# Reciprocal root of q, k and the convolution's norm as an exponential of a logarithm, in a hybrid conv / attention / expert block

## The chip, the core and the metric

The kernel runs on one core of one Trainium2 chip. The metric is the device time of one execution in microseconds, the median of several runs. One core has five engines that run their own instruction queues and meet at semaphores: PE (matrix products; PEld is its loading of weights), DVE (vectors), ACT (activations), POOL, and SP, which here only issues DMAs. Reads and writes of the on-chip tiles are fast; `bank` tiles are the eight accumulation banks that PE writes.

## What is computed

One layer of a streaming encoder over 512 tokens of width 2048, all in f32. Cut to what matters here:

```python
h   = rmsnorm(x, norm1_g) * (1 + scale1) + shift1
a   = h @ w_in
# group A: GLU -> causal depthwise conv(31) -> layernorm -> silu, 1024 channels
h   = conv(val * sigmoid(gate)) + dw_b
y   = (h - mean(h)) * rsqrt(var(h) + EPS);  conv_out = silu(y * g + b)
# group B: 8 heads; q and k are 128 plain columns and 64 rotary columns per head
q = rmsnorm(q, q_norm_g);  k = rmsnorm(k, k_norm_g)     # x * rsqrt(mean(x*x) + EPS) * g
q, k = rope(q), rope(k)
p = softmax(mask(q @ k.T * 192**-0.5));  attn_out = p @ v
x = x + gate1 * (concat[conv_out, attn_out] @ w_out)
# then: norm, product-key search for 16 of 16384 experts in each of 8 heads,
# gelu(x . u) of the experts chosen, and the weighted sum of their v rows
```

## The kernel before

Features lie on partitions and tokens along a row, so most tiles are 128x512. Each f32 product is made of three passes on PE: a weight tile `w_raw` comes by DMA, ACT copies it to `w_hi` (L430), DVE subtracts to get `w_lo` (L761), and PE multiplies `w_hi` by the high and low part of the activations and `w_lo` by the high part (L1294, L1295, L1296). The order of the work is written out by hand for each engine; nothing reorders it, and every wait is a semaphore in the code.

The stages follow each other: modulation vectors and the first norm, the input projection, the convolution's taps on DVE, the values and rotary parts, then the **attention stage** (from 545 to 790 us of the span), the output projection, the expert keys, and from there to the end the stream of all expert weights. The change touches the attention stage alone.

Its start (call it the prelude): PE sums the convolution's channels into `bank3`, projects q and k of head 0 (`project`), sums the squares of q and k across partitions with a product with ones (`sum_squares`, L1394, L1396, L1398), projects head 1, sums the squares of the centred convolution (L1460), and then the squares of q and k of head 1. After each sum ACT takes a square root (`root_of`, L544, for q as r = 0 and k as r = 1; L595 for the convolution) and DVE the reciprocal (`norm_of`, L922; L1000 for the convolution, late), and multiplies `q_n`, `q_r`, `k_n` and `k_r` by it (L924, L927, L930). PE may overwrite the bank of q only after `q_used`, which `q_n` sets.

Then one **head** after another, eight of them. In each, PE writes the scores of four query blocks (L1411, L1412), DVE takes the row maximum (L936 to L938), ACT the exponential (L554), DVE the division by the sum (L944), PE transposes the result (L1418), DVE copies the transposed block out of `bank7` (L951), but the fourth block is copied by ACT (L572), and PE multiplies the values by the whole (`weigh_values`, L1426), which ACT copies to `att_o` (L576). Between the blocks of heads 1 to 6 (in order of time) PE projects q and k of the head two further on. At the end of each of these six heads ACT does `root_of(0)`, then the copy L572 for which `weigh_values` waits, then `root_of(1)`, then L576:

```python
root_of(0, v, j)
act.wait_ge(tr_ready, ...)
act.activation(prob_t[:, :, 3 * P:4 * P], bank[7]..., ACT.Copy)   # L572
root_of(1, v, j)
act.wait_ge(pv_ready, ...)
act.activation(att_o[:, u + i * 2, :], bank[4][:], ACT.Copy)      # L576
```

DVE does the norm of q at the very end of a head and the norm of k after the first block of the next. The last two heads have no projection; the seventh still has a norm of k.

ACT holds the tables of one set of functions at a time. Where the next function is in another set, an ACT_TABLE_LOAD stands ahead of it, put there when the program is built.

Of the kernel before, what the change touches and what calls it, by code (L numbers as in the profile page):

```python
# [9 lines left out]
ALU = mybir.AluOpType  # L10
ACT = mybir.ActivationFunctionType
# [11 lines left out]
CONV_CH, CONV_W = 1024, 31  # L23
# [4 lines left out]
NLAT = KQ + KKV  # L28
# [57 lines left out]
def build(nc, x_d, c_d, pos_d, prm_d, wada_d, win_d, wqr_d, wval_d, whd_d, wout_d, wwq_d, keys_d, u_d, v_d, urow_d, out_d):  # L86
# [4 lines left out]
    with ExitStack() as ctx:  # L91
# [10 lines left out]
        bank = [ctx.enter_context(nc.psum_tensor(f"bank{i}", [P, T], F32)) for i in range(8)]  # L102
# [22 lines left out]
        qr_rot = at("qr_rot", 194, [P, 4, T])  # L125
        cos_t = at("cos_t", 204, [P, T])
        sin_t = at("sin_t", 206, [P, T])
        root = at("root", 208, [P, T])
        rstd = at("rstd", 210, [P, T])
# [3 lines left out]
        q_r = [at("q_r0", 132, [P, T]), at("q_r1", 202, [P, T])]  # L133
        k_r = [at("k_r0", 134, [P, T]), at("k_r1", 180, [P, T])]
        v_s = [at(f"v_s{s}", 160 + 2 * s, [P, T]) for s in range(2)]
        qk_root = [at(f"qk_root{s}", 136 + 6 * s, [P, T]) for s in range(2)]
        qk_rstd = [at("qk_rstd0", 204, [P, T]), at("qk_rstd1", 206, [P, T])]
# [80 lines left out]
        eps_c, pidx, pidx_i = tiny[:, 0:1], tiny[:, 1:2], at("pidx_i", 218.5, [P, 1], I32)  # L218
# [16 lines left out]
        sq_ready, sq_used, sum_ready, root_ready, rstd_ready = (sem(n) for n in ("sq_ready", "sq_used", "sum_ready", "root_ready", "rstd_ready"))  # L235
# [3 lines left out]
        lat_scaled, lat_hi, lat_lo = sem("lat_scaled"), sem("lat_hi"), sem("lat_lo")  # L239
# [184 lines left out]
        def _(act):  # L424
# [115 lines left out]
            def root_of(r, u, i):  # L540
                act.wait_ge(ssq_ready, 2 * u + r + 1 + i * 4)
                if not first_of_all(r, u, i):
                    act.wait_ge(hrstd_ready, 2 * u + r - 1 + i * 4)
                act.activation(qk_root[r][:], bank[2 + r][:], ACT.Sqrt, bias=eps_c,  # L544
                               scale=1.0 / (NOPE + ROPE)).then_inc(hroot_ready, 1)

            def exps(qb, u, i):
                w, s = (qb + 1) * P, qb % 2
# [43 lines left out]
                act.wait_ge(sq_used, KD + NLAT + k - 1)  # L592
                act.activation(sq[k % 2][:], conv_o[:, k, :], ACT.Square).then_inc(sq_ready, 1)
            act.wait_ge(var_sum, 1)
            act.activation(root[:], bank[2][:], ACT.Sqrt, bias=eps_c, scale=1.0 / CONV_CH).then_inc(root_ready, 1)  # L595
            for r in range(2):
                root_of(r, 1, 0)
            with act.Fori(0, 2) as i:
# [17 lines left out]
            for k in range(NC_T):  # L616
                act.wait_ge(ln_scaled, k + 1)
                act.activation(conv_o[:, k, :], conv_o[:, k, :], ACT.Silu, bias=pcol("ln_b", k),
                               scale=pcol("ln_g", k)).then_inc(ln_silu, 1)
# [134 lines left out]
        def _(dve):  # L754
# [161 lines left out]
            def norm_of(r, u, i):  # L916

                r0, r1 = 64 * u, 64 * u + 64
                dve.wait_ge(hroot_ready, 2 * u + r + 1 + i * 4)
                if not (isinstance(i, int) and u + i == 0):  # L920
                    dve.wait_ge(qk_ready, u + i * 2)
                dve.reciprocal(qk_rstd[r][:], qk_root[r][:]).then_inc(hrstd_ready, 1)  # L922
                dve.wait_ge(hrstd_ready, 2 * u + r + 1 + i * 4)
                dve.scalar_tensor_tensor(out=(q_n, k_n)[r][u][:], in0=bank[r][:], scalar=pcol(("qn_g", "kn_g")[r]), in1=qk_rstd[r][:],  # L924
                                         op0=ALU.mult, op1=ALU.mult).then_inc((q_used, k_used)[r], 1)
                if r == 0:
                    T_.step(dve.tensor_tensor(q_r[u][r0:r1, :], qr_rot[r0:r1, i, :], qk_rstd[0][r0:r1, :], ALU.mult))  # L927
                    dve.wait_ge(q_used, u + 1 + i * 2)
                else:
                    dve.tensor_tensor(k_r[u][r0:r1, :], kr_rot[r0:r1, :], qk_rstd[1][r0:r1, :], ALU.mult).then_inc(qk_ready, 1)  # L930
# [64 lines left out]
                    dve.tensor_tensor(conv_o[:, k, :], conv_o[:, k, :], rstd[:], ALU.mult).then_inc(ln_scaled, 1)  # L995

            head(0, 3, (1, 3), None, lambda: (ada_mid(31), lo(J_OUT + 1)))
            dve.wait_ge(root_ready, 4)
            dve.wait_ge(centred, NC_T)
            dve.reciprocal(rstd[:], root[:]).then_inc(rstd_ready, 1)  # L1000
            dve.wait_ge(rstd_ready, 4)
            head(1, 3, None, None, lambda: ln_scale(0))
            ln_scale(4)
# [667 lines left out]
```

## Time and profile before

| | us |
|---|---|
| median of 3 runs | 3591.26 (3589.4 to 3591.8) |
| the profiled execution | 3590.57 |
| its span, first to last instruction | 3588.8 |
| PE busy | 3294.2 (92%) |
| DVE busy | 2623.4 (73%) |
| ACT busy | 1100.9 (31%) |

The span is cut into stages of very different kinds, so the shares say little of one of them. The attention stage is 245 us of it. A row of the timeline gives start, duration, engine, line, operation and tiles, and in brackets how long the engine had been idle and what ended that. The granted clock of PE is 1.00 at its upper level, 2.4 GHz, and 0.50 at its lower one, 1.2 GHz.

### The profile page before, as it was taken

Reading aid. Unit: us, or ns where it says so; the run is one execution under the profiler, and the core shown is the slowest. Engines: PE = TensorE matmul, PEld = TensorE weight load, DVE = VectorE, ACT = ScalarE, POOL = GpSimd, SP = SyncE. Lnnn points to the kernel's source line nnn. Section 1 sums busy time; section 2 is a strip of 40 time slices with the busy share of each in tenths; the row PEclk is TensorE's granted clock in tenths of the full one; section 3 lists DMA queues with packets and bytes.
Section 4 is the critical chain, followed back from the end, with each engine's and each line's share of the span. In section 5 each row is a group of like instructions: output and inputs, shape, how many; then the busy total and the mean of one; then the engine's idle time right before and its main releaser. Section 6 shows DMA issues by size and latency. Waiting matters only on the chain.

```text
span 3588.8 us, 46376 instructions
## 1 busy us (share of the span) xinstructions
PE 3294.2 (92%) x17301; PEld 3009.1 (84%) x17301; DVE 2623.4 (73%) x3074; ACT 1100.9 (31%) x1015; POOL 652.4 (18%) x428
## 2 busy tenths in 40 slices
PE   1598888879989999999999999999999998999999
PEld 0386764447757799999999999999999998999999
DVE  6868986865463488888777777774777777677777
ACT  2123124341122344444322323322333332233332
POOL 0200000000020002222102221120433333233333
PEclk7599989979979999999999999999999999999999
DMA  8572221225423437777647777776999998999997
GB/s 352 215 288 88 93 70 63 85 81 212 186 107 142 168 145 294 273 280 270 242 174 285 264 280 301 274 281 253 358 342 348 348 345 310 359 347 350 343 348 289
DMA packets 241085, 883.48 MB, mean 246 GB/s; under 512 B 17680, under 2 KB 132496, under 8 KB 169744
## 3 DMA queue, kind: packets, MB, share of 16 engines
q1 hardware_dynamic: 161552, 545.82, 41.2%
q0 software_dynamic: 55296, 268.46, 20.0%
q10 hardware_dynamic: 24192, 68.64, 5.1%
q8 instruction: 23, 0.38, 0.0%
q14 instruction: 22, 0.18, 0.0%
HBM read 824.13 MB, written 58.72 MB: 246 GB/s over the span
## 4 chain that ended last, share of the span: by engine, by line
PE 64%; DVE 20%; DMA 6%; issue 5%; ACT 4%; DVEq 1%; SPq 0%; POOL 0%; ACTq 0%; PEldq 0%
PE bank L1595 9%; PE bank L1596 9%; PE bank L1597 9%; PE bank L1294 9%; PE bank L1296 9%; PE bank L1295 9%; DVE u_row L1125 3%; ACT w_hi L430 3%; DVE tap_a L893 2%; DMA w_raw<-wwq 2%; PE bank L1570 2%; DVE tap_b L893 2%; DMA ada_w<-wada 2%; DVE w_lo L761 2%; PE bank L1486 2%
## 5 line engine op out<-in xcount | busy, mean ns | idle before, releaser
L761 DVE TENSOR_TENSOR w_lo<-w_raw,w_hi 128x2048 fp32r<-128x2048 f32 (+1 forms) x327 | 742.2, 2270 | 783.1 <-ACT w_hi L430 771.5
L1294 PE MATMUL bank<-act_hi,w_hi 128*128 128x384 f32 (+1 forms) x2840 | 1031.2, 363 | 176.7 <-POOL act_lo L402 106.8
L430 ACT ACTIVATE w_hi<-w_raw 128x2048 fp32r<-128x2048 f32 (+1 forms) x327 | 621.9, 1902 | 1547.2 <-PE bank L1296 824.5
L1295 PE MATMUL bank<-act_lo,w_hi 128*128 128x384 f32 (+1 forms) x2840 | 1014.5, 357 | 0.0
L1296 PE MATMUL bank<-act_hi,w_lo 128*128 128x384 f32 (+1 forms) x2840 | 1013.9, 357 | 0.0
L1294 PEld LDWEIGHTS bank<-act_hi,w_hi 128*128 128x128 f32 x2840 | 548.0, 193 | 244.6 <-issue 144.1
L1595 PE MATMUL bank<-wt_hi,w_hi 128*128 128x384 f32 x2048 | 688.3, 336 | 16.7 <-DVEq L1255 9.0
L1597 PE MATMUL bank<-wt_hi,w_lo 128*128 128x384 f32 x2048 | 686.2, 335 | 0.0
L1596 PE MATMUL bank<-wt_lo,w_hi 128*128 128x384 f32 x2048 | 686.2, 335 | 0.0
L1296 PEld LDWEIGHTS bank<-act_hi,w_lo 128*128 128x128 f32 x2840 | 547.4, 193 | 34.7
L1295 PEld LDWEIGHTS bank<-act_lo,w_hi 128*128 128x128 f32 x2840 | 549.0, 193 | 30.3 <-issue 0.2
L420 POOL DMA_INDIRECT v_row<-v,vrow_i x256 | 388.0, 1516 | 749.8 <-DVE y_g L1240 672.6
L413 POOL DMA_INDIRECT u_row<-u_rows,urow_i x128 | 219.3, 1714 | 1185.2 <-DVE u_row L1125 860.1
L1595 PEld LDWEIGHTS bank<-wt_hi,w_hi 128*128 128x128 f32 x2048 | 386.3, 189 | 19.0 <-DVEq L1255 9.4
L1596 PEld LDWEIGHTS bank<-wt_lo,w_hi 128*128 128x128 f32 x2048 | 386.2, 189 | 0.0
L1597 PEld LDWEIGHTS bank<-wt_hi,w_lo 128*128 128x128 f32 x2048 | 386.1, 189 | 0.0
L1240 DVE SCALAR_TENSOR_TENSOR y_g<-v_row,gate_g,y_g 128x1024 f32<-128x1024 f32 x256 | 327.5, 1279 | 14.7 <-DVE y_g L1240 4.2
L1125 DVE SCALAR_TENSOR_TENSOR u_row<-u_row,h2t 128x2048 f32<-128x2048 f32 x128 | 288.6, 2285 | 0.1
L402 POOL TENSOR_TENSOR act_lo<-X,act_hi 128x512 fp32r<-128x512 f32 x32 | 43.4, 1357 | 983.8 <-ACT act_hi L443 983.8
L728 ACT ACTIVATE wt_hi<-wt 128x1536 fp32r<-128x1536 f32 x64 | 95.5, 1492 | 266.8 <-DVE wt L1213 266.7
L1570 PE MATMUL bank<-hot,hot 128*128 128x128 bf16 x1152 | 144.1, 297 | 15.8 <-DVE hot L1203 15.8
L1570 PEld LDWEIGHTS bank<-hot,hot 128*128 128x128 bf16 x1152 | 128.5, 117 | 28.8 <-issue 26.9
(232 smaller groups left out, 2632.5 us busy)
## 6 DMA issues: line engine op xcount, KB each, us to landing
w_raw<-u SPq DMA_DIRECT2D x128, 1024.0 KB
w_raw<-v SPq DMA_DIRECT2D x128, 1024.0 KB
ada_w<-wada SPq DMA_DIRECT2D x80, 1024.0 KB, 5.3
gelu_l<-gelu_scratch SPq DMA_DIRECT2D x64, 768.0 KB
gate_l<-gate_scratch SPq DMA_DIRECT2D x64, 768.0 KB
w_raw<-win SPq DMA_DIRECT2D x27, 1024.0 KB
gelu_scratch<-gelu_s ACTq DMA_DIRECT2D x128, 192.0 KB, 6.8
gate_scratch<-g_chunk ACTq DMA_DIRECT2D x8, 3072.0 KB, 12.4
```

The lines of the kernel that those rows point to most:

```text
L420: pool.indirect_dma_start(v_row[n % 4][:], None, rows_of_v, bass.IndirectOffsetOnAxis(ap=vrow_i[:, n % P:n % P + 1], axis=0), element_offs ...
L430: act.activation(w_hi[n0 % 2][:, 0:width], w_raw[n0 % 2][:, 0:width], ACT.Copy).then_inc(hi_done, 1)
L761: dve.tensor_tensor(w_lo[s][:, 0:width], w_raw[s][:, 0:width], w_hi[s][:, 0:width].bitcast(F32), ALU.subtract).then_inc(lo_done, 1)
L1125: dve.scalar_tensor_tensor(out=row, in0=row, scalar=1.0, in1=h2t, op0=ALU.mult, op1=ALU.mult, accum_out=col).then_inc(dots_done, 1)
L1240: dve.scalar_tensor_tensor(out=acc, in0=v_row[m % 4][:], scalar=gate_g[:, bass.ds(turn * 8 + m, 1)], in1=acc, op0=ALU.mult, op1=ALU.add).t ...
L1294: pe.matmul(out, wh, hi_t(k), start=(k == 0), stop=False)
L1295: pe.matmul(out, wh, lo_t(k), start=False, stop=False)
L1296: last = pe.matmul(out, wl, hi_t(k), start=False, stop=(k == nk - 1))
L1570: last = pe.matmul(o, hot2[:, u, g, :, q], hot1[j][:, u, g, :, q], start=(j == 0), stop=(j == 2))
L1595: pe.matmul(o, w_hi[s][:, col], th, start=(start and e == 0), stop=False)
L1596: pe.matmul(o, w_hi[s][:, col], tl, start=False, stop=False)
L1597: last = pe.matmul(o, w_lo[s][:, col], th, start=False, stop=(stop and e == 1))
```

## The change

The root on ACT becomes a logarithm, and a second ACT instruction takes the exponential of minus half of it, which is the reciprocal root. DVE's reciprocal goes. This is done for the 16 norms of q and k and for the convolution's norm; the norms of x and of the latents keep the root and the reciprocal. ACT's exponential waits until the tile that it writes has been used; DVE multiplies `q_r` ahead of `q_n` now, so that `q_used` stands for both.

```diff
             def root_of(r, u, i):
...
-                act.activation(qk_root[r][:], bank[2 + r][:], ACT.Sqrt, bias=eps_c,
+                act.activation(qk_root[r][:], bank[2 + r][:], ACT.Ln, bias=eps_c,
                                scale=1.0 / (NOPE + ROPE)).then_inc(hroot_ready, 1)
+                act.wait_ge(hroot_ready, 2 * u + r + 1 + i * 4)
+                act.wait_ge((q_used, qk_ready)[r], u + i * 2)
+                act.activation(qk_rstd[r][:], qk_root[r][:], ACT.Exp, scale=-0.5).then_inc(hrstd_ready, 1)
...
-            act.activation(root[:], bank[2][:], ACT.Sqrt, bias=eps_c, scale=1.0 / CONV_CH).then_inc(root_ready, 1)
+            act.activation(root[:], bank[2][:], ACT.Ln, bias=eps_c, scale=1.0 / CONV_CH).then_inc(root_ready, 1)
+            act.wait_ge(root_ready, 4)
+            act.wait_ge(lat_scaled, NLAT)
+            act.activation(rstd[:], root[:], ACT.Exp, scale=-0.5).then_inc(rstd_ready, 1)
...
             def norm_of(r, u, i):
...
-                dve.wait_ge(hroot_ready, 2 * u + r + 1 + i * 4)
+                dve.wait_ge(hrstd_ready, 2 * u + r + 1 + i * 4)
...
-                dve.reciprocal(qk_rstd[r][:], qk_root[r][:]).then_inc(hrstd_ready, 1)
-                dve.wait_ge(hrstd_ready, 2 * u + r + 1 + i * 4)
+                if r == 0:
+                    T_.step(dve.tensor_tensor(q_r[u][r0:r1, :], qr_rot[r0:r1, i, :], qk_rstd[0][r0:r1, :], ALU.mult))
...
             head(0, 3, (1, 3), None, lambda: (ada_mid(31), lo(J_OUT + 1)))
-            dve.wait_ge(root_ready, 4)
             dve.wait_ge(centred, NC_T)
-            dve.reciprocal(rstd[:], root[:]).then_inc(rstd_ready, 1)
             dve.wait_ge(rstd_ready, 4)
```

Three lines come in on ACT ahead of the heads' code, so that its lines have other numbers now (L572 is L575, L554 is L557, L576 is L579). The built program's order on ACT at the end of a head, in the loop's body, before:

```order
L554 ACTIVATE prob_97,tiny<-bank,tiny 128x512
L541 REGISTER_ALU
L544 ACT_TABLE_LOAD
L544 ACTIVATE qk_root_92<-bank,tiny 128x512
L571 REGISTER_ALU
L572 ACTIVATE prob_t<-bank 128x4x128
L541 REGISTER_ALU
L544 ACTIVATE qk_root_93<-bank,tiny 128x512
L575 REGISTER_ALU
L576 ISA
L576 ACTIVATE att_o<-bank 128x512
L554 ACT_TABLE_LOAD
```

And of the change, the same place:

```order
L544 ACT_TABLE_LOAD
L544 ACTIVATE qk_root_92<-bank,tiny 128x512
L548 ACT_TABLE_LOAD
L548 ACTIVATE qk_rstd_94<-qk_root_92 128x512
L574 REGISTER_ALU
L575 ACTIVATE prob_t<-bank 128x4x128
L541 REGISTER_ALU
L544 ACT_TABLE_LOAD
L544 ACTIVATE qk_root_93<-bank,tiny 128x512
L548 ACT_TABLE_LOAD
L548 ACTIVATE qk_rstd_95<-qk_root_93 128x512
L578 REGISTER_ALU
```

Ahead of the copy into `prob_t` stands one table load and one activation more than before, and behind it two loads and one activation more; the load ahead of the next head's first exponential (L554) is gone. In the whole stage 14 loads become 34.

On DVE, the norm of q of head 0 in the prelude (and of k behind it), before:

```order
L922 RECIPROCAL qk_rstd_94<-qk_root_92 128x512
L924 SCALAR_TENSOR_TENSOR q_n_82<-bank,prm,qk_rstd_94 128x512
L927 TENSOR_TENSOR q_r_86<-qr_rot,qk_rstd_94 64x512
L922 RECIPROCAL qk_rstd_95<-qk_root_93 128x512
L924 SCALAR_TENSOR_TENSOR k_n_84<-bank,prm,qk_rstd_95 128x512
```

And of the change:

```order
L929 TENSOR_TENSOR q_r_86<-qr_rot,qk_rstd_94 64x512
L930 SCALAR_TENSOR_TENSOR q_n_82<-bank,prm,qk_rstd_94 128x512
L930 SCALAR_TENSOR_TENSOR k_n_84<-bank,prm,qk_rstd_95 128x512
L935 TENSOR_TENSOR k_r_88<-kr_rot,qk_rstd_95 64x512
```

Both reciprocals are gone, and `q_r` has moved ahead of `q_n`.

## Rows read from the trace of the kernel before

**Rows 1.** The page's head.
```profile
span 3588.8 us, 46376 instructions
```

**Rows 2.** Groups by line: operation and shapes, count, busy us, mean ns, idle before.
```profile
L922 DVE RECIPROCAL qk_rstd<-qk_root 128x512 f32<-128x512 f32 x16 | 53.6, 3350 | 17.4 <-ACT qk_root L544 17.4
...
L544 ACT ACT_TABLE_LOAD x7 | 9.0, 1283 | 0.5 <-PE bank L1396 0.4
L554 ACT ACT_TABLE_LOAD x7 | 9.0, 1283 | 0.1
...
L459 ACT ACTIVATE sin_t<-sin_t 128x512 f32<-128x512 f32 x1 | 0.6, 630 | 24.1 <-DVE sin_t L812 24.1
```

**Rows 3.** ACT's timeline at the end of the fifth head.
```profile
711.53 1.28 ACT L544 ACT_TABLE_LOAD   x1
712.83 0.69 ACT L544 ACTIVATE qk_root<-bank,tiny 128x512 f32<-128x512 f32 x1
713.77 0.60 ACT L572 ACTIVATE prob_t<-bank 128x512 f32<-128x512 f32 x1 [0.25 <-PE bank L1418]
714.26 0.68 ACT L544 ACTIVATE qk_root<-bank,tiny 128x512 f32<-128x512 f32 x1
718.57 0.60 ACT L576 ACTIVATE att_o<-bank 128x512 f32<-128x512 f32 x1 [3.63 <-PE bank L1426]
```

**Rows 4.** PE's timeline from there, and its wait in the fourth head.
```profile
677.85 0.50 PE L1294 MATMUL bank<-act_hi,w_hi 128*128 128x512 f32 x1 [0.33 <-DVE k_n L924]
...
713.08 0.66 PE L1418 MATMUL bank<-ident,prob 128*128 128x128 f32 x4 [1.24 <-DVE prob L944]
714.42 4.12 PE L1426 MATMUL bank<-prob_t,v_s 128*128 128x512 f32 x8 [0.69 <-ACT prob_t L572]
718.37 0.39 PE L1411 MATMUL bank<-k_n,q_n 128*128 128x128 f32 x2
```

**Rows 5.** DVE's timeline at the start of the sixth head.
```profile
719.35 0.11 DVE L936 MEMSET bank<- 64x64 f32 x1 [1.08 <-PE bank L1412]
```

**Rows 6.** PE's weighing of the values in the third and in the last head.
```profile
667.28 2.42 PE L1426 MATMUL bank<-prob_t,v_s 128*128 128x512 f32 x8 [0.69 <-ACT prob_t L572]
...
783.67 4.63 PE L1426 MATMUL bank<-prob_t,v_s 128*128 128x512 f32 x8 [0.69 <-ACT prob_t L572]
```

**Rows 7.** Windows of 1 us: length, busy PE, PEld, DVE, ACT, POOL, clock, DMA, GB/s.
```profile
714.00:715.00 1.00, 0.58 (x1) 0.30 (x2) 1.00 (x1) 0.94 (x2) 0.00 (x0) 0.85 0.45 188
715.00:716.00 1.00, 1.00 (x2) 0.33 (x1) 1.00 (x1) 0.00 (x0) 0.00 (x0) 0.50 0.00 0
```

**Rows 8.** Timeline of the prelude, DVE.
```profile
563.67 3.35 DVE L922 RECIPROCAL qk_rstd<-qk_root 128x512 f32<-128x512 f32 x1 [1.67 <-ACT qk_root L544]
...
590.33 3.35 DVE L922 RECIPROCAL qk_rstd<-qk_root 128x512 f32<-128x512 f32 x1 [12.35 <-ACT qk_root L544]
```

**Rows 9.** Timeline of the prelude, PE.
```profile
567.96 0.76 PE L1294 MATMUL bank<-act_hi,w_hi 128*128 128x512 f32 x1 [4.74 <-DVE q_n L924]
...
598.98 0.80 PE L1294 MATMUL bank<-act_hi,w_hi 128*128 128x512 f32 x1 [5.80 <-DVE w_lo L761]
```

**Rows 10.** Timeline of the prelude, ACT.
```profile
586.85 0.69 ACT L595 ACTIVATE root<-bank,tiny 128x512 f32<-128x512 f32 x1 [1.31 <-PEq L1463]
589.61 0.69 ACT L544 ACTIVATE qk_root<-bank,tiny 128x512 f32<-128x512 f32 x1 [2.08 <-PE bank L1396]
```

**Rows 11.** DVE's timeline in the seventh head.
```profile
746.10 3.34 DVE L922 RECIPROCAL qk_rstd<-qk_root 128x512 f32<-128x512 f32 x1
...
751.28 0.11 DVE L936 MEMSET bank<- 64x64 f32 x1
...
757.38 0.11 DVE L936 MEMSET bank<- 64x64 f32 x1
```

**Rows 12.** PE's timeline in the seventh head.
```profile
747.15 0.91 PE L1412 MATMUL bank<-k_r,q_r 64*128 64x384 f32 x2
...
755.01 2.07 PE L1412 MATMUL bank<-k_r,q_r 64*128 64x512 f32 x2
```

More of the change, by code:

```diff
@@ L926, in norm_of @@
                 if r == 0:
-                    T_.step(dve.tensor_tensor(q_r[u][r0:r1, :], qr_rot[r0:r1, i, :], qk_rstd[0][r0:r1, :], ALU.mult))
                     dve.wait_ge(q_used, u + 1 + i * 2)
```

## The prediction

> **What bounds the kernel now.** I read the page first for the span [rows 1], then the groups by line for the prices of what goes and what comes [rows 2], and then, since only the attention stage is touched, the timelines of ACT, PE and DVE side by side through one head of it. The fifth head stands for six that look alike. What the reader is to see there is who is waited for at its end. PE has transposed the last block; ACT is free to copy it at 713.77, only 0.25 us after its root of q ended [rows 3]; PE starts to weigh the values 0.69 us behind its own last work, released by that copy, and the next head's scores follow at once, at 718.37 [rows 4]. DVE takes the first maximum of the next head at 719.35, having waited 1.08 us for PE's scores [rows 5]. So PE sets the pace of these heads, and at one place in each it hangs on ACT: on the copy that stands in ACT's queue behind the root of q. DVE's reciprocals run beside PE's products. They are on the path at three other places: twice in the prelude, where PE waits for `q_n` and later for a `w_lo` that stands behind a norm of q in DVE's queue [rows 9], and once in the seventh head, which has no projection for PE.
>
> **What goes, what comes.** DVE loses 17 reciprocals of 3.35 us, 57 us of work [rows 2, 8]. ACT gets 17 exponentials of 128x512; the nearest row is the sine from and to on-chip tiles, 0.63 us [rows 2], so 10.7 us. The logarithm I price as the root that it replaces, 0.69 us [rows 3]: same shapes, same bias; no row shows a logarithm. Logarithm and exponential are in different sets in the built program, so every pair has two table loads: 34 where there were 14, at 1.283 us each [rows 2], 25.7 us more. What matters is where they stand.
>
> **The end of each of six heads.** Now: load 711.53, root 712.83 to 713.52, copy 713.77 when the transposed block was there [rows 3]. Changed: load, logarithm to 713.52, load 713.54 to 714.82, exponential 714.83 to 715.46. The copy can start some 0.1 us ahead of that end, as the root of k at 714.26 did ahead of the copy's end at 714.37 [rows 3]: at 715.36. That is 1.59 us later, and PE, whose wait for this copy ends last (0.69 us, [rows 4]), starts to weigh 1.59 us later. Behind the copy come two more loads and an exponential: load 715.96, logarithm 717.25, load 717.95, exponential to 719.87. They lie beside the weighing, whose end moves from about 718.5 to 720.1, so that `att_o` waits for PE as now, but with 0.3 us to spare where it had 3.63 [rows 3]. The next head's first exponential no longer has a load of 1.28 us ahead of it [rows 2]; PE does not wait for it, having a whole projection to do. So **+1.59 in six heads: +9.5 us**. Nothing of the 3.35 us that DVE gets back twice per head is seen: its norm of q is ready sooner, but it then waits longer for PE's scores; its norm of k frees the bank of k earlier, which PE waited for only once in earnest, 0.33 us in the fourth head [rows 4].
>
> **The prelude.** The first norm of q: root to 563.57, reciprocal 563.67 to 567.02, `q_n` to 567.81, PE released at 567.96 [rows 8, 9]. Changed: logarithm to 563.57, load to 564.87, exponential to 565.50, then `q_r` (0.67) and `q_n` (0.75) to 567.06: PE 0.75 us earlier, and with it all that follows, up to the convolution's root at 586.85 [rows 10], whose load fits between ACT's last square and the end of the sum. Behind that root come a load, an exponential and a load again, on ACT alone (PE needs only the logarithm): from 586.78, 1.28 + 0.63 + 1.28 gives 590.03 for the logarithm of q of head 2, where the root stood at 589.61 [rows 10]. Then 0.69, 1.28 and 0.63 to 592.67, `q_r` and `q_n` to 594.2; DVE's next work was at 595.22 before (590.33 + 3.35 and the two products, [rows 8]). So DVE is 1.0 us ahead when it turns to the `w_lo` for which PE waited until 598.98 [rows 9]. **-1.0 us** for the whole prelude, in which the 0.75 is contained.
>
> **The seventh head.** DVE runs from 746.10 without a gap to the maximum of the third block at 751.28 [rows 11]. Without the 3.35 us it would be there at 747.93, but PE ends that block's scores only at 747.15 + 0.91 = 748.06 [rows 12], so at about 748.2. The fourth block: DVE's maximum at 757.38 would come at 754.3; PE's scores, which ended at 757.08 while they had 0.3 us to spare, hang on DVE's division two steps ahead and move with it. **-3.1 us**. The convolution's reciprocal at the end of this head goes too, at nothing: DVE waits over 3 us there for PE.
>
> **The clock of PE.** In five of the six heads the clock falls to its lower level while the values are weighed: 0.85 granted in 714 to 715, 0.50 in the next [rows 7], after PE had twice stood idle ahead of it, 1.24 us and 0.69 us [rows 4]. The weighing then takes 4.0 to 4.1 us. In the third head it stayed up and took 2.42 [rows 6]. With 1.59 us more of idle time ahead of it I expect it to fall in the third head too: +1.7, of which the 0.33 us of waiting for `k_n` that follow come back: +1.4. For the other five it may go either way. The low stretch may start within the longer wait, where it costs nothing: 1.59 us at half speed is 0.8 a head, -4.0. Or the weighing may take 4.63 as in the last head, all of it low [rows 6]: 0.5 a head, +2.5. I take the middle, -0.7. **Together +0.7 us**, between -4.0 and +4.2.
>
> **The sum.** 9.5 - 1.0 - 3.1 + 0.7 = +6.1 us. On the profiled execution, whose span is 3588.8 us [rows 1] and whose time 3590.57, this gives 3596.7. The median of the runs is 0.7 us above that execution, so 3591.26 + 6.1 = **3597.4**. Behind the attention stage the weights come through rings of two buffers, so the delay goes through to the end. With the bounds of the clock this case spans 3592.7 to 3600.9; the exponential between 0.60 and 0.69 moves it by 0.4.
>
> **A rule of the pages, and a row against it.** In these rows a table load starts 0.01 us behind the instruction ahead of it, lasts 1.28 us, and the activation starts 0.01 us behind it [rows 3]. The Trainium skill (ScalarE: Activation LUTs, What ACT_TABLE_LOAD costs) gives 1283 ns for the load, which the trace agrees with, and a drain of 1380 ns beside it, 2.66 us for every switch, which this trace doesn't show. The same page (Table sets: the hidden batching unit) says that one set holds exponential and logarithm both, so that a logarithm followed by an exponential needs one load; the built program shows two.
>
> **Rivals.** (1) *A switch costs more than its load.* If each load that follows a working ACT cost as much again, 1.3 us more, the copy would be late by that again in six heads: +8, 3605. The rows of 14 loads speak against it. The drain of the page ScalarE: Activation LUTs of the Trainium skill would be this. 0.04. (2) *The clock stays low for longer*, the one that ends slower. The copy's lateness makes PE idle for 2.28 us instead of 0.69, close behind another 1.24. If that brings a second low stretch over the projection, each costs what one costs in the weighing, 4.12 - 2.42 = 1.7: in all six heads +10, 3607; in three, 3602. It decides from the point where the scores at the next head's start still run at 0.50. Against it: the clock was up again at the scores every time, even behind the 4.74 us without work ahead of 567.96 it was back some 3 us later. 0.10. (3) *The low stretch goes away* from the weighing (it falls into the wait, or comes only in the next idle time): the clock's term is then -1.7 in five heads instead, 9.5 - 1.0 - 3.1 - 8.5 = -3.1, 3588; with part of it, about 3592. The third head speaks for it, where the same waits left the clock up. 0.10. (4) *The change doesn't do what it says*: were logarithm and exponential in one set as loaded, the exponential of q would end at 712.85 and the copy would not move; heads 0, prelude -4.9 (the first norm 2.1 earlier, the second 2.8), seventh head -3.1: 3583. This is the case of the one set in the sentence above; the order of the built program has the loads, which is why it gets 0.04.
>
> **How the numbers follow.** Forecast 0.68, the four rivals 0.04, 0.10, 0.10, 0.04, and 0.04 for what I don't see. 0.2% of 3591 is 7.2 us, about what a measurement of this kernel can tell from no change: faster ends below 3584.1, slower begins at 3598.4. The forecast's own range lies mostly below 3598.4; I give 0.20 of its 0.68 to slower. Slower: 0.20 + 0.04 + 0.10 + 0.03 = 0.37. Faster: 0.04 + 0.01 = 0.05. Same: 0.58. The range goes from 3592 to 3603: the forecast's span and the milder part of rival 2, which leaves out rival 1, rival 4 and the ends of 2 and 3.
>
> **What would show it.** In the profile after, ACT at the end of a head: load, logarithm, load, exponential, and the copy 1.6 us behind the last transposition; PE's wait ahead of the weighing 2.3 us instead of 0.69; `att_o` right behind the weighing. Each of the heads 1 to 6 should be some 1.6 us longer, and in the seventh the maximum of the third block should come 2.1 us behind the start of the k norm instead of 5.2. The granted clock should be at 0.50 once in each. The prediction is wrong if the exponential or the logarithm has another length than 0.63 and 0.69, if loads cost more when they follow each other closely, or if the copy was not the last thing that PE waited for.

## The result and the profile after

| | before | after |
|---|---|---|
| median of 10 runs each, same session | 3589.44 | 3603.06 |
| lowest to highest | 3586.73 to 3592.1 | 3596.76 to 3606.07 |
| profiled execution | 3590.57 | 3597.68 |
| its span | 3588.8 | 3595.9 |

The ratio is 1.0034, with a 95% interval of 1.0025 to 1.0042: the change makes the kernel slower, by 9 to 15 us. The forecast had said +6.1 us and called it most likely (0.58, against 0.37 for slower) within the 0.2% that a measurement can tell from nothing. It is more, and outside. The ratios in this text are taken over all runs of both kernels, so they don't follow from the two medians to the last digit (here 3603.06 / 3589.44 would be 1.0038).

The page after, head and engines. Against [rows 1], DVE has lost the 57 us of reciprocals and ACT has gained 36:

```profile
span 3595.9 us, 46412 instructions
PE 3297.2 (92%) x17301; PEld 3008.6 (84%) x17301; DVE 2566.4 (71%) x3057; ACT 1137.3 (32%) x1052; POOL 669.2 (19%) x428
```

ACT's groups by line (count, busy us, mean ns, idle before). They answer to [rows 2]: L544 is the logarithm now and L548 the exponential.

```profile
L544 ACT ACT_TABLE_LOAD x16 | 20.5, 1283 | 0.7 <-PE bank L1399 0.4
L548 ACT ACT_TABLE_LOAD x16 | 20.5, 1283 | 0.3
L544 ACT ACTIVATE qk_root<-bank,tiny 128x512 f32<-128x512 f32 x16 | 11.0, 687 | 0.2
L548 ACT ACTIVATE qk_rstd<-qk_root 128x512 f32<-128x512 f32 x16 | 10.1, 630 | 0.2
```

All three prices held: 0.69 us for the logarithm, 0.63 for the exponential, 1.283 for a load, and with one of each for the convolution there are 34 loads. Then ACT's timeline at the end of the fifth head, the place of [rows 3] (start, duration, engine, line, operation, and in brackets the idle time before):

```profile
721.77 1.28 ACT L544 ACT_TABLE_LOAD   x1
723.07 0.69 ACT L544 ACTIVATE qk_root<-bank,tiny 128x512 f32<-128x512 f32 x1
723.77 1.28 ACT L548 ACT_TABLE_LOAD   x1
725.07 0.63 ACT L548 ACTIVATE qk_rstd<-qk_root 128x512 f32<-128x512 f32 x1
725.60 0.58 ACT L575 ACTIVATE prob_t<-bank 128x512 f32<-128x512 f32 x1
...
730.03 0.58 ACT L579 ACTIVATE att_o<-bank 128x512 f32<-128x512 f32 x1
```

And PE's and DVE's beside it, the places of [rows 4] and [rows 5]:

```profile
723.32 0.66 PE L1421 MATMUL bank<-ident,prob 128*128 128x128 f32 x4 [1.24 <-DVE prob L949]
726.23 3.41 PE L1429 MATMUL bank<-prob_t,v_s 128*128 128x512 f32 x8 [2.26 <-ACT prob_t L575]
729.44 0.64 PE L1414 MATMUL bank<-k_n,q_n 128*128 128x128 f32 x2
```
```profile
730.95 0.11 DVE L941 MEMSET bank<- 64x64 f32 x1 [3.75 <-PE bank L1415]
```

The copy stands where the forecast had put it, behind the exponential, and PE's wait ahead of the weighing is 2.26 us instead of 0.69. It is so in all six heads. DVE, with its norm of q done early, waits 3.75 us for PE's scores where it waited 1.08 us [rows 5]: what it was freed of has become idle time. What the forecast had not looked for is in the last PE row: these scores take 0.64 us where they took 0.39 [rows 4], since PE runs at its lower clock there.

The attention stage, from PE's first sum over the convolution's channels to the first product of the output projection, as one window each (length; busy PE, PEld, DVE, ACT, POOL; granted clock; DMA share; GB/s), before and after:

```profile
545.30:790.94 245.64, 197.57 (x609) 109.11 (x609) 178.64 (x295) 91.36 (x156) 0.00 (x0) 0.87 0.18 66
```
```profile
544.33:802.59 258.26, 205.35 (x608) 113.77 (x609) 122.66 (x278) 127.64 (x193) 0.00 (x0) 0.85 0.17 63
```

So the stage is 12.6 us longer, and 7.8 us of that is PE *busy* time, for the same products: 197.6 to 205.4. Waiting alone can't do that; a lower clock can, and the granted clock is 0.85 where it was 0.87. The whole stage, taken apart at marks that both traces have:

| piece of the stage | before | after | difference |
|---|---|---|---|
| start to the release of head 1's projection by `q_n` | 22.66 | 21.97 | -0.7 |
| from there to the sum of the convolution's squares | 11.09 | 11.12 | 0.0 |
| that sum (L1460, now L1463) | 7.67 | 9.31 | +1.6 |
| end of that sum to PE's release by `w_lo` | 12.26 | 12.01 | -0.25 |
| from there to the first weighing | 19.88 | 22.57 | +2.7 |
| five heads, weighing to weighing | 119.79 | 130.64 | +10.85 |
| sixth weighing to seventh | 24.28 | 20.90 | -3.4 |
| seventh to eighth | 20.74 | 23.10 | +2.4 |
| from there to the end | 7.27 | 6.64 | -0.6 |

These add up to 12.6. The wait explains 6 x 1.57 = 9.4, the exponentials in the place of reciprocals -0.9 in the prelude and -3.1 in the seventh head. The remaining 7.2 us I put down to the clock; as a remainder it is near the 7.8 us of longer busy time. It is 1.6 in the convolution's sum, 2.7 - 1.57 = 1.1 in the first head, 10.85 - 5 x 1.57 = 3.0 in the next five, and 1.5 in the last pieces. The profiled execution gives some 5 us of it back: the lag behind before is 12.8 us at 1300 us of the span, 8.1 at 2500 and 7.1 at its end, in stages that the change doesn't touch. That isn't the change's doing: in the second pair of profiles (below) nothing is given back, and the lag is 13.9, 16.2 and 15.4 us at the same places. The median of ten runs is 13.6 us above before's.

### The profile page after: what moved, and what is told of

Read it like the earlier page. It is cut to its first block, busy times and chain, and to the rows that moved or that the text cites. A ratio compares the mean times of both kernels' runs of the same rounds, so it can differ in the third digit from the quotient of the medians.

```text
span 3595.9 us, 46412 instructions
## 1 busy us (share of the span) xinstructions
PE 3297.2 (92%) x17301; PEld 3008.6 (84%) x17301; DVE 2566.4 (71%) x3057; ACT 1137.3 (32%) x1052; POOL 669.2 (19%) x428
## 4 chain that ended last, share of the span: by engine, by line
PE 64%; DVE 19%; DMA 6%; issue 5%; ACT 4%; DVEq 0%; SPq 0%; POOL 0%; ACTq 0%; PEldq 0%
PE bank L1598 9%; PE bank L1599 9%; PE bank L1600 9%; PE bank L1297 9%; PE bank L1299 9%; PE bank L1298 9%; DVE u_row L1128 3%; ACT w_hi L430 3%; DVE tap_a L899 2%; DMA w_raw<-wwq 2%; PE bank L1573 2%; DVE tap_b L899 2%; DVE w_lo L767 2%; DMA ada_w<-wada 2%; PE bank L1491 1%
## 5 line engine op out<-in xcount | busy, mean ns | idle before, releaser
L420 POOL DMA_INDIRECT v_row<-v,vrow_i x256 | 403.1, 1575 | 733.7 <-DVE y_g L1243 652.5
```

The lines of the kernel that those rows point to most:

```text
L420: pool.indirect_dma_start(v_row[n % 4][:], None, rows_of_v, bass.IndirectOffsetOnAxis(ap=vrow_i[:, n % P:n % P + 1], axis=0), element_offs ...
```

## The experiments

Two theories of the copy's place stood against each other. By the first, the time comes from the *lateness of one ACT instruction*, the copy for which PE waits. By the second it comes from *ACT's total work*, 36 us more in the stage, wherever it stands (the texts of what was expected call them theory A and theory B). A third question was where the clock's share comes from. Each kernel was run beside the kernel before on the same chip; its median was 3588.3 for the first four kernels below, 3588.7 for the change again, the change filled and the grouped and filled one, 3587.6 for the kernel before filled and the one with the prelude filled.

**Copy first.** The changed kernel with its copy moved ahead of the logarithm; ACT does exactly the same work.

```diff
-                if v is not None:
-                    root_of(0, v, j)
                 act.wait_ge(tr_ready, LEAD + 4 * u + 4 + i * 8)
                 act.activation(prob_t[:, :, 3 * P:4 * P], ...).then_inc(pt_ready, 1)
                 if v is not None:
+                    root_of(0, v, j)
                     root_of(1, v, j)
```

> The changed kernel with the ACT copy of the fourth transposed block moved ahead of the logarithm of q, so that no table load stands between the transposition and the weighing; all 34 loads stay. If the copy's lateness is the cost (theory A), PE's wait ahead of the weighing falls from 2.26 us back to 0.69 in all six heads, 9.4 us go and what the idle time did to the clock goes too: between 4 us faster than the kernel before and equal to it. If it is the work on ACT as such (theory B: 34 loads, late att_o, late first exponential), it stays 10 us or more slower than before, since ACT does as much and att_o is even 3.6 us later.

Measured: 3591.94, ratio 1.0004 (0.9995 to 1.0013). ACT's copy, and PE's weighing behind it, in its fifth head:

```profile
718.25 0.60 ACT L573 ACTIVATE prob_t<-bank 128x512 f32<-128x512 f32 x1 [2.26 <-PE bank L1421]
```
```profile
718.90 2.42 PE L1429 MATMUL bank<-prob_t,v_s 128*128 128x512 f32 x8 [0.69 <-ACT prob_t L573]
```

ACT now waits for PE instead of PE for ACT, PE's wait is back to 0.69 us in all six heads, and 10 to 11 us of the change's cost are gone with ACT's work unchanged. As an account of those 10 us the second theory falls. But it isn't wholly wrong, and here the expectation, no slower than before, missed something (the median is 3.6 us above before's, though the interval takes in no difference). With the copy first, the norm of q is later still, and in three heads PE waits for `q_n` ahead of its projection, 1.42, 1.34 and 1.22 us, which neither before nor the change has; in the seventh head ACT is still busy with the norms when the first block's exponential is due, and PE waits 4.92 us for that block instead of 1.63:

```profile
724.44 0.47 PE L1297 MATMUL bank<-act_hi,w_hi 128*128 128x512 f32 x1 [1.22 <-DVE q_n L930]
...
751.90 0.48 PE L1421 MATMUL bank<-ident,prob 128*128 128x128 f32 x1 [4.92 <-DVE prob L949]
```

These are 4.0 and 3.3 us that ACT's longer queue costs in this order; the 3.1 us of the seventh head are lost by it (24.3 us from the sixth weighing to the seventh, as before). The clock in the prelude stays too (the convolution's sum still takes 9.2 us), and so does the piece from the seventh to the eighth weighing (23.05).

**Load before the copy.** The opposite test: the kernel before, reciprocals and all, with one exponential of a single column between its root of q and its copy. It writes a spare column that nothing reads.

```diff
                     root_of(0, v, j)
+                    act.activation(tiny[:, 10:11], eps_c, ACT.Exp)
```

> The kernel before, roots and reciprocals as they were, with one exponential of a single column put between the root of q and the copy in each of six heads, which brings a table load of 1.28 us ahead of it and one ahead of the root of k. Theory A: the copy comes about 1.2 us later (load 1.28, column 0.2, less 0.25 of slack), six times 7.2, and some us more from the clock: +7 to +12. If only the reciprocals' removal from DVE or the exponential of 512 columns mattered: 0.

Measured: 3594.43, ratio 1.0021 (1.0012 to 1.0030), 6.1 us over before by the medians and 7.5 by the ratio, the lower end of what was expected. ACT at the end of its fifth head, and PE's weighing:

```profile
720.31 1.28 ACT L571 ACT_TABLE_LOAD   x1
721.60 0.20 ACT L571 ACTIVATE tiny<-tiny 128x1 f32<-128x1 f32 x1
721.71 0.58 ACT L573 ACTIVATE prob_t<-bank 128x512 f32<-128x512 f32 x1
```
```profile
722.34 3.96 PE L1427 MATMUL bank<-prob_t,v_s 128*128 128x512 f32 x8 [1.83 <-ACT prob_t L573]
```

The wait is 1.83 us, 1.14 longer than before; six of them are 6.8 us, close to what was measured. One table load in the wrong place, with no other part of the change, costs about half of what the change costs. This run also answers rival 1: a switch that costs more than its load would have made the wait longer than 1.28 + 0.2 allow. The Trainium skill (ScalarE: Activation LUTs, What ACT_TABLE_LOAD costs) puts a drain of 1380 ns beside the load; here, as in the trace before, the next activation starts 0.01 us behind the load, and the trace disagrees with it.

**Both logarithms, then both exponentials.** The changed kernel with its work on ACT grouped by function, so that a head needs two loads instead of four and the copy has only one ahead of it.

```diff
-                    root_of(0, v, j)
+                    log_of(0, v, j)
                 act.wait_ge(tr_ready, LEAD + 4 * u + 4 + i * 8)
                 act.activation(prob_t[:, :, 3 * P:4 * P], ...).then_inc(pt_ready, 1)
                 if v is not None:
-                    root_of(1, v, j)
+                    log_of(1, v, j)
+                    for r in range(2):
+                        exp_of(r, v, j)
```

> The changed kernel with both logarithms of a head taken under one table load, on either side of the copy, and both exponentials behind the copy under one load; the prelude as changed. 14 loads in the heads' part fewer than 34 by 12. Theory A: as with the copy first, PE's wait is 0.69 us, the norm of q reaches DVE when its reciprocal used to end, the seventh head keeps its 3.1 us: 2 to 4 us faster than before, or equal to it if the prelude costs what it did in the profile of the change (+1.7). Theory B: half of the extra loads gone, so half of the loss stays, +6.

Measured: 3586.53, ratio 0.9991 (0.9982 to 1.0001). ACT at the end of its fifth head:

```profile
708.65 1.28 ACT L544 ACT_TABLE_LOAD   x1
709.94 0.69 ACT L544 ACTIVATE qk_root<-bank,tiny 128x512 f32<-128x512 f32 x1
710.89 0.60 ACT L581 ACTIVATE prob_t<-bank 128x512 f32<-128x512 f32 x1 [0.25 <-PE bank L1429]
711.38 0.68 ACT L544 ACTIVATE qk_root<-bank,tiny 128x512 f32<-128x512 f32 x1
712.08 1.28 ACT L550 ACT_TABLE_LOAD   x1
713.38 1.15 ACT L550 ACTIVATE qk_rstd<-qk_root 128x512 f32<-128x512 f32 x2
```

The idea of the change, a root without a reciprocal, costs no time in this order that could be measured: the load ahead of the exponentials is the one that the next head's softmax needs anyway, as in the kernel before. Four of the five heads take 22.5 us where before's take 24.2, because the clock stays up in them; whether that is owed to the grouping, this run alone does not tell, and the next one speaks against it: there the clock stays up in five of six heads with the roots and waits of before. Its stage is 4.6 us shorter than before's, but the gain of the medians, 1.8 us, is not one that can be told from nothing.

**The convolution's norm alone.** The kernel before with only this norm as an exponential of a logarithm.

```diff
-            act.activation(root[:], bank[2][:], ACT.Sqrt, bias=eps_c, scale=1.0 / CONV_CH).then_inc(root_ready, 1)
+            act.activation(root[:], bank[2][:], ACT.Ln, bias=eps_c, scale=1.0 / CONV_CH).then_inc(root_ready, 1)
+            act.wait_ge(root_ready, 4)
+            act.wait_ge(lat_scaled, NLAT)
+            act.activation(rstd[:], root[:], ACT.Exp, scale=-0.5).then_inc(rstd_ready, 1)
```

> The kernel before with only the convolution's norm as logarithm and exponential. ACT then has, behind the logarithm, a load, the exponential and a load for the root of q: 590.8 us instead of 589.6 on the timeline of before, on the path to the w_lo that PE waits for. Expected +1.2 us by my step; nothing from the reciprocal at the seventh head's end, which stood in idle time. If the prelude is bound elsewhere: 0.

Measured: 3589.38, ratio 1.0003 (0.9994 to 1.0012): the total tells nothing. The step does: from the end of the convolution's sum to PE's release by `w_lo` it takes 13.45 us instead of 12.26, +1.19, and PE waits 6.98 us there instead of 5.80 [rows 9]. But the sum itself takes 9.1 us, though PE's waits ahead of it are as before (4.73 and 2.45 us). And the five heads, which this edit doesn't touch, take 116.1 us where before's take 119.8: PE waits 1.24 and 0.69 us ahead of each weighing as before, and the clock falls in one of six. So these waits alone don't bring the low clock. The sum's group by line, and that of the kernel with the load before its copy, whose prelude is before's too:

```profile
L1461 PE MATMUL bank<-sq,ones 128*128 128x512 f32 x16 | 9.1, 717 | 2.5 <-ACT sq L593 2.5
```
```profile
L1461 PE MATMUL bank<-sq,ones 128*128 128x512 f32 x16 | 7.7, 616 | 2.5 <-ACT sq L594 2.5
```

**Both kernels again**, for their spread from run to run.

> The changed kernel again, for a second profile and its time beside the others on one chip. The copy's part (2.26 us of wait in six heads) must be the same to 0.1 us; what differs between this profile and the first is the clock. Total near 3603, 0.3 to 0.4% above before; a stage between 250 and 260 us.

> The kernel before again, for a second profile of the attention stage. It was 245.6 us in the first, with the clock low in the weighing of five of six heads. If the clock's falls are luck in place, the stage differs by some us here and the waits do not.

Measured: the change 3600.41 (six runs), ratio 1.0031 (1.0019 to 1.0044), its stage 255.66; before 3587.73 in a single run, its stage 244.97 (the interval compares the change with all the runs of before beside it). So the stages differ by 12.6 and by 10.7 us in two pairs, of which 5.4 are waits and steps that are equal in both, and the clock is 7.2 and 5.3. PE's wait ahead of the weighing is 2.26 in all twelve heads, 0.69 in all twelve of before. The convolution's sum takes 9.17 us in the second profile of the change, 7.67 in the second of before.

**PE's waits filled, changed kernel.** If the clock's share comes from PE standing idle, work that nobody reads should bring it back. Products of tiles that are there anyway are put ahead of the last transposition and ahead of the weighing, into the bank that the weighing overwrites, in all eight heads.

```diff
+            def fill(n):
+                for _ in range(n):
+                    pe.matmul(bank[4][:], act_hi[:, 0, 0:P], act_hi[:, 1, :], start=True, stop=True)
...
             def weigh_values(u, i):
...
-                pe.wait_ge(att_ready, LEAD + u + i * 2)
...
+                pe.wait_ge(att_ready, LEAD + u + i * 2)
+                fill(4)
                 turn_probs(3, u, i)
+                fill(8)
                 weigh_values(u, i)
```

> The changed kernel with products that nobody reads put into PE's two waits at the end of each head: 4 of 128x512 ahead of the last block's transposition (0.23 us each) and 8 ahead of the weighing, into the bank that the weighing then overwrites. They fit into the waits of 1.24 and 2.26 us. If idle time of PE ahead of the weighing is what brings the low clock into it, the weighing takes 2.4 us instead of 3.4 to 4.6 in the six heads, and the kernel is 6 to 10 us faster than the change without them (near 3593, +1 to +5 against before), though the copy is as late as ever. If the low clock has another cause, the time is that of the change, +13.

Measured: 3583.44, ratio 0.9985 (0.9976 to 0.9994): 17 to 20 us under the change, about twice what was expected. PE at the end of its fifth head:

```profile
714.89 0.66 PE L1421 MATMUL bank<-ident,prob 128*128 128x128 f32 x4 [0.31 <-DVE prob L949]
715.30 2.08 PE L1426 MATMUL bank<-act_hi 128*128 128x512 f32 x8
717.81 2.42 PE L1432 MATMUL bank<-prob_t,v_s 128*128 128x512 f32 x8 [0.42 <-ACT prob_t L575]
```

The copy is as late as in the change, yet each weighing takes 2.42 us, and the heads 24.1 us, which is the 22.53 of a head at the upper clock plus the 1.57 of the copy's lateness. So the two shares are told apart: in the change a head takes 26.13 us on average, 1.57 from the wait and 2.0 from the clock. In the kernel before it is 23.96, 1.4 from the clock. That the clock cost something before the change already is one reason why the expectation was too small. It isn't the whole: in the profiles the stage is 13.8 and 11.2 us shorter than in the two of the change, and the rest of the 17 to 20 lies in later stages, which the edit doesn't touch; that part stays unexplained.

**The same in the kernel before**, with `fill(4)` and `fill(2)`, the shorter wait needing less.

> The kernel before, with 4 and 2 unread products in PE's waits of 1.24 and 0.69 us at the end of each head. The filled change ran at 24.10 us a head with the weighing at full clock; if the copy's lateness is 1.57 us and nothing else differs, the filled kernel before runs at 22.53 us a head, and is 5 to 9 us faster than the filled change (3583.4): 3575 to 3579, 0.997 of before. If part of the 1.57 came from the clock, the heads here are longer than 22.6.

Measured: 3580.01, ratio 0.9976 (0.9967 to 0.9985). So the gain of filling is not the change's merit. The expectation, 3575 to 3579, was missed by 1 us, and the gain over the filled change is 3.4 us where 5 to 9 were expected. Its heads take 22.6 to 23.3 us, not 22.53 throughout. PE now meets the norm of k that DVE finishes late, in four places; one of them:

```profile
654.99 0.50 PE L1294 MATMUL bank<-act_hi,w_hi 128*128 128x512 f32 x1 [0.70 <-DVE k_n L924]
```

**Grouped and filled.** The grouped kernel with `fill(4)` and `fill(2)`, and with the convolution's exponential moved behind head 2's norms.

> The batched version (both logarithms of a head under one load, both exponentials under another behind the copy), with the convolution's exponential moved behind those of head 2 in the prelude, so that the logarithm of q has no load ahead of it and the norm of q comes 2.6 us earlier than in the change (a load, an exponential and a load less), and with 4 and 2 unread products in PE's waits of 1.24 and 0.69 us. Batched was 0.9991 of before. The prelude should give 2.6 us more, the clock up to 1.7 in each head where it fell: 8 to 14 us faster than before, 0.996 to 0.998.

Measured: 3573.57, ratio 0.9960 (0.9946 to 0.9973), faster than both kernels and than the one above by 6.4 us. All its heads take 22.55 us, and no PE row in them waits for `k_n`. Here the reciprocals' absence is worth something: 114.8 - 112.8 = 2.0 us in five heads, with the clock up. In the kernel before, at its own clock, only 0.33 us of it could show [rows 4]. The seventh head adds 2.75 us (20.39 against 23.14). What the new order of the prelude adds was not run by itself. Against before beside it this kernel is 14 to 15 us faster, the upper end of what was expected.

**The prelude filled, changed kernel.** Only the two long waits of the prelude, by 15 and 20 such products, and nothing in the heads.

```diff
+            pe.wait_ge(rope_done, 5)
+            fill(15)
             for r in range(2):
                 project(r, 1, 0)
...
             pe.wait_ge(rope_done, 5)
+            fill(20)
             with pe.Fori(0, 3) as i:
```

> The changed kernel with unread products in PE's two long waits of the prelude alone: 15 (3.4 us) ahead of head 2's projections and 20 (4.6 us) ahead of head 1's first scores; the heads as changed. If idle time brings the low clock into the prelude, the sum of the convolution's squares takes 7.7 us again instead of 9.2 to 9.3, the low stretches over both projections go, and the kernel is 4 to 5 us faster than the change, near 3597, ratio 1.0015 to 1.0022 of before. If the 9.3 us have another cause (the order of ACT's work), they stay, and so does the time.

Measured: 3588.38, ratio 1.0005 (0.9996 to 1.0014): 12 to 15 us under the change (11 to 13, each counted from the kernel before beside it), where 4 to 5 were expected. PE at the two places of [rows 9], and the convolution's sum:

```profile
567.73 0.47 PE L1297 MATMUL bank<-act_hi,w_hi 128*128 128x512 f32 x1 [0.59 <-DVE q_n L930]
...
596.93 0.50 PE L1297 MATMUL bank<-act_hi,w_hi 128*128 128x512 f32 x1 [0.96 <-DVE w_lo L767]
```
```profile
L1469 PE MATMUL bank<-sq,ones 128*128 128x512 f32 x16 | 7.7, 616 | 2.5 <-ACT sq L596 2.5
```

PE is released by `w_lo` 51.17 us behind the stage's start instead of 54.41, so the prelude alone is 3.2 us shorter, and no low clock is left in it. More comes from the heads: they still wait 2.26 us each, but take 25.5 to 25.7 us where the change's take up to 27.0. In all, the stage is 9.1 and 6.5 us shorter than in the two profiles of the change. That the gain is more than the prelude's 3.2 us is shown by the intervals. That the filling of the prelude steadied the clock in the heads, up to 150 us later, is not shown: it rests on one profile, and heads differ by as much within one profile of the change.

**All the weighings together.** The twelve profiles have 72 ends of a head (six in each). How often the granted clock was at 0.50 in the wait ahead of the weighing or in the weighing:

| PE's waits ahead | profiles | low |
|---|---|---|
| 1.24 and 0.69 | before twice, convolution alone, copy first, grouped | 5, 5, 1, 2, 2 of 6 |
| 1.24 and 1.83 | load before the copy | 4 of 6 |
| 1.24 and 2.26 | the change twice, prelude filled | 6, 6, 6 of 6 |
| filled | the change, before, grouped | 0, 0, 0 of 6 |

With 2.26 us the clock fell in 18 of 18, with the waits filled in none of 18, and with 0.69 in 15 of 30: there the wait leaves it open, and what decides isn't shown.

## Why the prediction was half right

The time, 3603.06, is where the stated range of 3592 to 3603 ends, 5.7 us from the forecast of 3597.4. The range had been drawn beyond the forecast's own bounds for a milder form of rival 2, and that is what came. There is some luck in it too: the forecast started from a median of three runs, 3591.26, where ten gave 3589.44, and the difference between the kernels, 13.6 us, is more than the 11.7 that the range allowed.

**The end of six heads, +9.5.** Right: 6 x (2.26 - 0.69) = 9.4. The copy came ahead of the exponential's recorded end as put, 725.60 against 725.70, `att_o` stood right behind the last exponential in the fifth head (730.03 against 729.49 + 0.63), and PE did not wait for the next softmax. Removing the lateness alone took 10 to 11 us away, adding a load alone brought 6.

**The prelude, -1.0.** The step on ACT and DVE was right: the release by `q_n` comes 0.7 us earlier, and from the convolution's sum to `w_lo` it is another 0.25. The step that failed is the sentence "and with it all that follows": between the two lies a stretch of PE, and it took 1.6 us longer. PE's clock by 1 us windows, after (PE idles until 577.42, then sums the squares):

```profile
577.00:578.00 1.00, 0.57 (x1) 0.50 (x2) 0.00 (x0) 0.80 (x2) 0.00 (x0) 0.66 0.00 0
578.00:579.00 1.00, 1.00 (x2) 0.34 (x1) 0.00 (x0) 0.00 (x0) 0.00 (x0) 0.50 0.00 0
579.00:580.00 1.00, 1.00 (x2) 0.34 (x1) 0.00 (x0) 0.43 (x1) 0.00 (x0) 0.50 0.00 0
580.00:581.00 1.00, 1.00 (x3) 0.43 (x2) 0.00 (x0) 0.20 (x1) 0.00 (x0) 0.63 0.00 0
```

In the kernel before the same stretch, from 579.05 on, is at 1.00 in every window:

```profile
579.00:580.00 1.00, 0.95 (x3) 0.50 (x4) 0.00 (x0) 0.42 (x1) 0.00 (x0) 1.00 0.00 0
580.00:581.00 1.00, 1.00 (x4) 0.25 (x2) 0.00 (x0) 0.63 (x1) 0.00 (x0) 1.00 0.00 0
```

I had counted the clock in the heads alone. There was a place in the prelude with waits of 4.74 and 2.5 us ahead of products, and it should have had a bound of its own: at half speed the sum's 7.67 us of products would take up to 7.67 more.

**The seventh head, -3.1.** Right. DVE's norm of k and the maxima of the third and fourth block:

```profile
759.16 0.74 DVE L930 SCALAR_TENSOR_TENSOR k_n<-bank,prm,qk_rstd 128x512 f32<-128x512 f32 x1
...
761.20 0.11 DVE L941 MEMSET bank<- 64x64 f32 x1 [0.25 <-PE bank L1415]
767.30 0.11 DVE L941 MEMSET bank<- 64x64 f32 x1
```

The third comes 2.04 us behind the start of the norm (forecast 2.1, before 5.18), the fourth 8.14 instead of 11.28, 3.1 us sooner [rows 11].

**The clock, +0.7 between -4.0 and +4.2.** This is the term that was mis-sized: 7.2 us in the profile shown, 5.3 in the second, beyond its own upper bound in both. (The bounds were not drawn alike: -4.0 leaves the third head out and +4.2 takes it at 1.7; with 1.4 for it on both sides they would have been -2.6 and +3.9.) Two steps of it failed. The first is "the low stretch may start within the longer wait, where it costs nothing". In the fourth head it does, and that head takes 25.53 us, 1.4 more than the 24.10 of a head with this wait and the clock up. But in the second and the third it starts there and does not end sooner for it: they take 26.70 and 26.94, 2.6 and 2.8 more. PE's windows through that weighing and the scores behind it:

```profile
673.00:674.00 1.00, 0.24 (x1) 0.24 (x2) 0.55 (x1) 0.98 (x3) 0.00 (x0) 0.50 0.00 0
...
678.00:679.00 1.00, 1.00 (x5) 0.78 (x5) 0.00 (x0) 0.47 (x1) 0.00 (x0) 0.50 0.00 0
679.00:680.00 1.00, 1.00 (x4) 0.65 (x4) 0.27 (x2) 0.12 (x1) 0.00 (x0) 0.64 0.00 0
```

Low from the wait through the weighing into the next head's scores. The second is the bound "all of it low, 4.63", which ended with the weighing; the low stretch runs over it, as rival 2 had named with its point of decision, "the scores at the next head's start still run at 0.50". It was that rival's mechanism in a milder form: in two of the six heads in either profile of the change (26.70 and 26.94; 26.82 and 27.04), at about 1 us more than the 1.7 of a low stretch over the weighing alone. That the clock would fall in the third head as well came true. In the six heads the term is 4.1 us (3.1 in the second pair), just inside the bound of 4.2. And 3.1 of the 7.2 us lay outside the six heads, where I had looked for none: in the convolution's sum and, in this profile, between the seventh and the eighth weighing. Of these the longer sum is in every profile whose q and k norms are changed and whose prelude is not filled (five of five besides the one shown), and with the convolution's norm alone, while the other is not steady: 23.10 us in one profile of the change, 20.91 in the other.

**The rivals.** A switch that costs more than its load is excluded by the row of the fifth head and by the load added alone. One set for logarithm and exponential did not come about: 34 loads. The low stretch did not go away in the change; that it can is shown by the filled kernels. The Trainium skill (ScalarE: Activation LUTs, Table sets: the hidden batching unit) says that one set has both functions and needs one load; the trace has a load ahead of each of the two in every pair, and in the grouped kernel too one stands between the logarithms and the exponentials.

**The total.** 9.4 - 0.9 - 3.1 + 7.2 = 12.6 in the stage, against a forecast of 9.5 - 1.0 - 3.1 + 0.7 = 6.1. Three terms held within 0.2 us; the fourth, an average between two bounds of which the upper was too narrow and left out the prelude, made the difference between "within 0.2%" and slower.

**What stays open.** What decides whether the clock falls in the convolution's sum. The kernel with only the convolution's norm changed has the same waits as before up to that sum (release by `q_n` at 22.69 us, wait 4.73) and yet has 9.1 us there, and the filled kernel before, with the sum starting at the same 34.17 us, has 7.67. So it is neither the 0.7 us by which the prelude moved nor a length of a wait alone. One pattern is left that no run separates: all seven profiles with a logarithm for the convolution and an unfilled prelude have 9.1 us or more, all four with a root have 7.67. Yet the logarithm's load starts 8 us behind the sum's first product, when the clock is up again, and in the kernel with only the convolution's norm changed ACT does the same ahead of the sum as in the kernel before. Nor was it tried whether filling the prelude of the grouped and filled kernel adds to its gain.

## What to carry to other kernels

Freeing an engine that nobody waits for buys little: look which instruction another engine waits for, and count what the edit queues ahead of *that* one, table loads first; then group by function, so that the loads merge. Don't only move the one instruction ahead: what is queued behind it gets later, and the copy moved first cost 4.0 and 3.3 us at the next waits. Give every wait of PE that an edit lengthens or shifts a clock term of its own, in every place where products stand behind it, with the bound reaching past the next products, not just to their end. And where PE idles for a short time in each round of a loop, try unread products in the wait: at 0.9976 with the kernel before it brought more than the change did in any order of its own (0.9991 at best).

## What the runs showed of the hardware

The clock costs time in short waits too. In the kernel before, PE stands idle 1.24 and 0.69 us ahead of a weighing, and the clock falls to its lower level, 1.2 GHz, in five of six heads; with these waits cut to 0.32 and 0.22 us by unread products all six weighings ran in 2.42 us instead of 4.1. The same two waits left the clock up in five of six heads of the kernel with only the convolution's norm changed, so they make the fall possible and not certain; 1.24 and 2.26 us brought it in 18 of 18. One low stretch in the change ran from PE's wait to the scores of the next head, nearly 7 us (672.9 to 679.7). And it isn't repeatable from run to run: the changed kernel's heads took 25.53 to 26.94 us in one profile and 25.55 to 27.04 in the other, in another order, while with its waits filled they took 24.09 to 24.15.

A copy on ACT from a bank can start before the activation ahead of it has its recorded end, by 0.1 us (725.60 against 725.07 + 0.63, 721.71 against 721.60 + 0.20), and is then recorded 0.58 us long instead of 0.60.
